# Three bfloat16 matmuls per token, of exact one-hots and split gates, in place of one float32 matmul

## The reference

```python
s1, i1 = lax.top_k(s[:, :, 0], PEER_TOPK)            # 16 best of 128 keys, first half
s2, i2 = lax.top_k(s[:, :, 1], PEER_TOPK)            # and second half
cand = (s1[..., :, None] + s2[..., None, :]).reshape(PEER_BLOCK, PEER_HEADS, PEER_TOPK * PEER_TOPK)
cidx = (i1[..., :, None] * PEER_NKEYS + i2[..., None, :]).reshape(PEER_BLOCK, PEER_HEADS, PEER_TOPK * PEER_TOPK)
top, pos = lax.top_k(cand, PEER_TOPK)
eidx = jnp.take_along_axis(cidx, pos, axis=-1)
gate = jax.nn.softmax(top, axis=-1)
a = jnp.einsum('thkd,td->thk', u_tab[eidx], xb).astype(jnp.float32)
act = (jax.nn.gelu(a) * gate).astype(xb.dtype)
return jnp.einsum('thk,thkd->td', act, v_tab[eidx])
```

## Time and profile before

| what | value |
|---|---|
| time, median of 3 runs | 1719.76 us (1716.88 to 1727.46) |
| profiled execution: span from the first to the last instruction | 1720.6 us |
| its mean granted TensorE clock | 0.990 of full speed |
| PE busy in it | 1674.9 us (97%) |
| DVE busy | 1178.9 us (69%) |
| POOL busy | 1124.5 us (65%) |

### The profile page before, as it was taken

The page is one execution under the profiler, slowest core; times in us unless marked ns, Lnnn a source line. Parts: engine busy times, 40 slices in busy tenths (PEclk is TensorE's granted clock), DMA queues, the critical chain, the costliest instruction groups (busy, mean ns, idle before and its releaser), DMA issues.

```text
span 1720.6 us, 27326 instructions
## 1 busy us (share of the span) xinstructions
PE 1674.9 (97%) x10559; PEld 1608.4 (93%) x10559; DVE 1178.9 (69%) x2324; ACT 665.7 (39%) x1059; POOL 1124.5 (65%) x677
## 2 busy tenths in 40 slices
PE   8999999899999999999999999999999999999996
PEld 3899878697999999999999999999999999999995
DVE  4340334645778799999787778446787887878755
ACT  2445222333334333334434433334444444444442
POOL 1677322132335888876766676778889799999952
PEclk9999999899999999999999999999999999999998
DMA  8544212034213999979999999979999999999951
GB/s 279 199 165 159 75 62 97 26 131 150 74 60 126 304 295 298 339 259 339 350 344 346 350 353 338 343 294 349 390 392 405 360 401 405 404 403 404 400 194 62
DMA packets 192705, 461.27 MB, mean 268 GB/s; under 512 B 21184, under 2 KB 99008, under 8 KB 192448
## 3 DMA queue, kind: packets, MB, share of 16 engines
q1 hardware_dynamic: 79872, 242.31, 39.4%
q0 software_dynamic: 46080, 167.79, 26.1%
q10 hardware_dynamic: 66624, 49.42, 8.7%
HBM read 407.64 MB, written 51.83 MB: 267 GB/s over the span
## 4 chain that ended last, share of the span: by engine, by line
PE 50%; DVE 4%; DMA 3%; POOL 1%; issue 1%; ACT 0%; DVEq 0%; SPq 0%; ACTq 0%
PE ps L922 44%; PE ps L933 5%; DMA tab<-in_tab 3%; POOL tLo L648 1%; DVE ug L1574 1%; POOL ug L658 0%; DVE ps L1584 0%; DVE yo L1820 0%; DVE eqb L1686 0%; DVE rs L1818 0%; DVE pick L1673 0%; DVE cand L1651 0%; DVE rs L1296 0%; DVE pos L1659 0%; PE ps L675 0%
## 5 line engine op out<-in xcount | busy, mean ns | idle before, releaser
L648 POOL TENSOR_TENSOR tLo<-tab,tHi 128x1024 fp32r<-128x1024 f32 x256 | 621.7, 2429 | 164.7 <-ACT tHi L1173 161.5
L1173 ACT CAST tHi<-tab 128x1024 fp32r<-128x1024 f32 x256 | 268.0, 1047 | 290.5 <-DMA tab<-in_tab 157.9
L922 PE MATMUL ps<-hHi,tLo 128*128 128x384 f32 x1024 | 352.0, 344 | 0.0
L922 PE MATMUL ps<-actHi,tLo 128*128 128x384 f32 x1024 | 342.7, 335 | 3.7 <-DVE actLo L1756 2.3
L922 PE MATMUL ps<-hHi,tHi 128*128 128x384 f32 x1024 | 345.7, 338 | 0.0
L922 PE MATMUL ps<-hLo,tHi 128*128 128x384 f32 x1024 | 344.8, 337 | 0.0
L922 PE MATMUL ps<-actLo,tHi 128*128 128x384 f32 x1024 | 342.1, 334 | 0.0
L922 PE MATMUL ps<-actHi,tHi 128*128 128x384 f32 x1024 | 342.1, 334 | 0.0
L636 POOL TENSOR_TENSOR wLo<-raw,wHi 128x1024 fp32r<-128x1024 f32 x53 | 128.2, 2418 | 292.1 <-ACT wHi L1004 292.1
L1574 DVE SCALAR_TENSOR_TENSOR ug<-ug,ps 128x1024 f32<-128x1024 f32 x160 | 191.0, 1218 | 48.3 <-DMA ug<-in_urows,eidx 47.1
L1584 DVE SCALAR_TENSOR_TENSOR ps<-ug,act_s,ps 128x1024 f32<-128x1024 f32 x158 | 202.5, 1282 | 5.0
(11 more groups left out here) (356 smaller groups left out, 2473.8 us busy)
## 6 DMA issues: line engine op xcount, KB each, us to landing
tab<-in_tab SPq DMA_DIRECT2D x256, 512.0 KB, 6.5
raw<-in_w SPq DMA_DIRECT2D x101, 512.0 KB, 3.7
gate_scratch<-stage ACTq DMA_DIRECT2D x48, 512.0 KB, 6.6
gt<-gate_scratch SPq DMA_DIRECT2D x32, 768.0 KB, 7.7
gelu_scratch<-ga ACTq DMA_DIRECT2D x112, 192.0 KB, 5.8
gin<-gelu_scratch SPq DMA_DIRECT2D x112, 192.0 KB, 11.0
ug<-in_urows,eidx POOLq DMA_INDIRECT x160, 6.7
ug<-in_vrows,eidx POOLq DMA_INDIRECT x160, 7.8
```

Source lines behind the costliest of these rows:

```text
L648: pool.tensor_tensor(tLo[:, n % SPL], tab[:, n % TABS], tHi[:, n % SPL].bitcast(F32), ALU.subtract).then_inc(s_tlo, 1)
L922: last = mm(ps[:, bank, 0:TD], w, x[:, k, 0:TD], start=first, stop=end)
L1173: nc.scalar.copy(tHi[:, n % SPL], tab[:, n % TABS]).then_inc(s_thi, 1)
```

## The change

The one-hots become bfloat16, in which 0, 1 and the key numbers are exact. Each gate is split into three bfloat16 pieces that add up to the float32 number (`gate3`; `gate_rest` holds what is left over). `w1` becomes `w3`, three products of `oh1` with a piece; PE adds the three matmuls of one token in PSUM. The layout of the one-hots turns from tokens x keys to keys x tokens, with the 8 tokens innermost, so that the operand that is repeated is repeated over the keys and its innermost run is 8 tokens. For PE the 128 columns of one token are therefore 8 elements (16 bytes) apart, in the weights and in the moving data; before they lay side by side. The key numbers (`key8`, repeated for 8 tokens), the chosen keys (`idx12`) and the gate pieces lie in SBUF now; nothing of the one-hots reads PSUM.

```diff
@@ gate_product (PE)
                     for t in range(4):
-                        last = mm(ps[:, GATE_BANKS[i % 3], t * P:(t + 1) * P], oh2[:, st % 2, 4 * part + t, :],
-                                  w1[:, st % 2, 4 * part + t, :], start=True, stop=True)
+                        for piece in range(3):
+                            last = mm(ps[:, GATE_BANKS[i % 3], t * P:(t + 1) * P], oh2[:, st % 2, :, 4 * part + t],
+                                      w3[:, st % 2, piece, :, 4 * part + t], start=(piece == 0), stop=(piece == 2))
                     last.then_inc(s_gmm, 1)
@@ preparation (DVE)
             for q in range(2):
                 nc.vector.tensor_copy(idx12[:, q], ps[:, 5 + q, 0:TD])
-            link(nc.vector.tensor_copy(oh1[:, 0:4, :], ps[:, 4, :].rearrange("p (t c) -> p t c", c=P)))
-            nc.vector.tensor_copy(iota_p, iota[:])
-            link(nc.vector.tensor_copy(g_cols[:], oh1[:, 0:3, :].rearrange("p t c -> p (t c)")))
+            nc.vector.tensor_copy(key8[:], over(iota[:], STEP_TOK))
+            link(nc.vector.tensor_copy(gate3[:, 0], ps[:, 4, 0:TD]))
+            link(tt(gate_rest[:], ps[:, 4, 0:TD], gate3[:, 0], ALU.subtract))
+            link(nc.vector.tensor_copy(gate3[:, 1], gate_rest[:]))
+            link(tt(gate_rest[:], gate_rest[:], gate3[:, 1], ALU.subtract))
+            link(nc.vector.tensor_copy(gate3[:, 2], gate_rest[:]))
@@ one_hots (DVE)
-                tt(oh2[:, st % 2], keys_, over(idx12[:, 1, at_], P), ALU.is_equal)
+                tt(oh2[:, st % 2], key8[:], along_keys(idx12[:, 1, at_]), ALU.is_equal)
                 if st:
                     v.wait_ge(s_oh, st)
-                link(tt(oh1[:], keys_, over(idx12[:, 0, at_], P), ALU.is_equal))
-                tt(w1[:, st % 2], oh1[:], over(g_cols[:, at_], P), ALU.mult).then_inc(s_oh, 1)
+                link(tt(oh1[:], key8[:], along_keys(idx12[:, 0, at_]), ALU.is_equal))
+                for piece in range(3):
+                    last = tt(w3[:, st % 2, piece], oh1[:], along_keys(gate3[:, piece, at_]), ALU.mult)
+                last.then_inc(s_oh, 1)
```

More of the change, by code:

```diff
@@ L280, in build @@
         ga = [at(f"ga{i}", [P, TD], (SPL_AT + 24576, SPL_AT + 24576 + 4 * TD, pos_sq + 6528)[i]) for i in range(3)]
-        idx12 = at("idx12", [P, 2, TD], SPL_AT + 27648)
+        gate3 = at("gate3", [P, 3, TD], SPL_AT + 27648, BF16)
         a_s = at("a_s", [P, NDOT], SPL_AT + 30720)
@@ L316, in build @@
         stage = peer("stage", [P, 2, NKEY, TB])
-        oh2 = peer("oh2", [P, 2, STEP_TOK, P])
-        w1 = peer("w1", [P, 2, STEP_TOK, P])
-        oh1 = at("oh1", [P, STEP_TOK, P], pos_sq + 1024)
+        gate_rest = at("gate_rest", [P, TD], zp[0])
+        oh2 = at("oh2", [P, 2, P, STEP_TOK], zp[0], BF16)
+        w3 = at("w3", [P, 2, 3, P, STEP_TOK], zp[0] + 4096, BF16)
+        oh1 = at("oh1", [P, P, STEP_TOK], pos_sq + 512, BF16)
+        key8 = at("key8", [P, P, STEP_TOK], pos_sq + 512 + 2048, BF16)
+        idx12 = at("idx12", [P, 2, TD], pos_sq + 512 + 4096, BF16)
+        assert 512 + 4096 + 4 * TD <= 3 * NST * PH * PK * 4
         zp[0] = Z_AT
@@ L350, in build @@
         h_rows = flat[:, 2 * 512:4 * 512]
-        g_cols = flat[:, 6 * 512:6 * 512 + TD]
-        iota_p = flat[:, 6 * 512 + TD:7 * 512]
         y_rows = h_rows
@@ L1720, in _, with along_keys @@
                 nc.vector.tensor_copy(idx12[:, q], ps[:, 5 + q, 0:TD])
-            link(nc.vector.tensor_copy(oh1[:, 0:4, :], ps[:, 4, :].rearrange("p (t c) -> p t c", c=P)))
-            nc.vector.tensor_copy(iota_p, iota[:])
-            link(nc.vector.tensor_copy(g_cols[:], oh1[:, 0:3, :].rearrange("p t c -> p (t c)")))
+            nc.vector.tensor_copy(key8[:], over(iota[:], STEP_TOK))
[4 more added lines that the diff above has]
+            link(nc.vector.tensor_copy(gate3[:, 2], gate_rest[:]))
             def one_hots(st):
                 at_ = slice(STEP_TOK * st, STEP_TOK * (st + 1))
-                keys_ = iota_p.unsqueeze(1).broadcast_to([P, STEP_TOK, P])
+                def along_keys(of_tokens):
+                    return of_tokens.unsqueeze(1).broadcast_to([P, P, STEP_TOK])
                 if st >= 2:
                     v.wait_ge(s_gmm, 2 * (st - 1))
-                tt(oh2[:, st % 2], keys_, over(idx12[:, 1, at_], P), ALU.is_equal)
+                tt(oh2[:, st % 2], key8[:], along_keys(idx12[:, 1, at_]), ALU.is_equal)
                 if st:
                     v.wait_ge(s_oh, st)
-                link(tt(oh1[:], keys_, over(idx12[:, 0, at_], P), ALU.is_equal))
-                tt(w1[:, st % 2], oh1[:], over(g_cols[:, at_], P), ALU.mult).then_inc(s_oh, 1)
+                link(tt(oh1[:], key8[:], along_keys(idx12[:, 0, at_]), ALU.is_equal))
+                for piece in range(3):
+                    last = tt(w3[:, st % 2, piece], oh1[:], along_keys(gate3[:, piece, at_]), ALU.mult)
+                last.then_inc(s_oh, 1)
             for st in range(NSTEP):
```

## The result

The changed kernel takes 1987.77 us (median of 6 runs, 1983.41 to 1996.11), the kernel before 1726.8 beside it: a ratio of 1.155, 95% interval 1.151 to 1.158. That is 188 us above the upper end of the range.

The account below looks back on a forecast made before the run. The prediction took PE's own work to bound the gate stage, its gate matmuls paced by weight loads. Profiled 1720.6 + 41.1 (gate matmuls) + 3.6 (start) = 1765.3 us, forecast 1765 us, range 1705 to 1800.

Parts of the forecast that it names:

- the price of a gate matmul: PE's gate steps: 24 bfloat16 matmuls at 0.107 us, 2.57 us in place of 1.71 a step, +41.1 us over 48.
- The gate matmuls are paced by their weight loads: PE's gate steps: loading 128 weight columns, not the columns that stream, sets the 0.107 us from one matmul to the next.
- rival A: PE's gate matmuls: bfloat16 weights load fast and 16-byte steps cost nothing; 0.060 us a matmul, 1711 us; chance 0.30.
- nearly half the rate: PE's 16-byte steps, priced from far-apart DVE output: half the rate for 128 columns taking 0.060 us is 0.12.
- Rival B: PE's gate matmuls: the layout slows the weight load itself to 0.214 us, +164 us, 1889 us; chance 0.12 (over 1800).
- 4.29 us a product: PE's product in a gate step: 4.29 us in the profile before, with no change to it in the sum.
- DVE's bfloat16 instructions: DVE's gate steps: five one-hot instructions at about 0.6 us, a step 5.4 us in place of 5.80, under PE's.
- D: DVE's one-hots miss the double rate as one operand is repeated: 8.1 us a step, 389 us; chance 0.12 with rival C.
- The preparation: DVE's work before the first gate step, with `key8` perhaps waiting for a POOL split: +3.6 us, once.
- PE didn't wait for DVE: Gate stage: PE waits for DVE's gate products at the first step, about 4 us, and hardly again.
- Rival C: Gate stage: POOL's splits hold up DVE's one-hots and make DVE the bound, +69 us, 1793 us; chance 0.12 with D.
- at least two hits per line: SBUF reads: full bandwidth wants two hits per 16-byte line; the new layout gives each column its own line; no price given.

Follow-up runs that it names:

- run 3: Changed kernel with only the weights read side by side, the moving data still 16 bytes apart (gates not the reference's): 1977.97 us.
- run 2: Changed kernel with only the moving data read side by side, the weights still 16 bytes apart (gates not the reference's): 1739.94 us.
- Run 1: Changed kernel with both weights and moving data read side by side (gates not the reference's): 1731.94 us, ratio 1.005 to the kernel before.
- 6: Changed kernel with the weights side by side and the moving columns 9 elements (18 bytes) apart in place of 8: 1982.32 us.
- 12: Changed kernel with every gate group cut in two, 12 matmuls behind the product and 12 in the middle of the next: 1976.66 us.
- 4: Changed kernel's computation with two tokens innermost, a token's columns 4 bytes apart in place of 16: 1737.09 us, ratio 1.0065 to the kernel before.
- 5: Changed kernel's computation with four tokens innermost, a token's columns 8 bytes apart in place of 16: 1774.53 us.
- run 7: Changed kernel's bfloat16 and three pieces with keys innermost: PE's columns side by side, DVE's repeated operand repeated in its innermost dimension: 1846.06 us.

## Why the prediction was wrong

**The step that failed is the price of a gate matmul**, "I take 0.107" with the upper end 0.214: it is 0.227, and 0.120 x 24 x 48 = 138 us of the error is that term. What the runs showed in its place: the moving data, read 16 bytes apart, set the pace (0.218 us with the weights side by side, run 3), and the weight load doesn't (0.063 with the weights alone apart, run 2). Both reasons behind it fell.

- "The gate matmuls are paced by their weight loads" fits the rows of the kernel before and was carried to bfloat16, where no row showed it. Run 1 has 24 loads at 0.055 us: bfloat16 loads of 128 columns hide under the streaming. That part of rival A was right. The Trainium skill ("TensorE: Matmul & The Clock Gate", Weight-path perf modes — Fast Weight Load (FWL) and DoubleRow) says that such loads go about twice as fast, and the 0.053 us that the prediction worked out from it as an estimate spoke against my 0.107. The trace of run 1, with a load and a matmul every 0.055 us, agrees.
- The layout was priced by a ratio. I read from the earlier trace rows that far-apart elements go at "nearly half the rate" and doubled the 0.060 us of a matmul. The same rows hold an absolute price, 1.8 ns an element; 128 of those are 0.23 us, and 1.77 ns a moving column was measured. That the two are one mechanism isn't shown, as the earlier trace rows are a DVE output with a step of 64 bytes and this is PE's input with 16; that the numbers come so near may be luck. But as an upper end it was the better choice, and the ratio had nothing to show that it carries over to PE.

Rival B had about the right number (0.214) for the wrong reason: it gave the slowness to the weight load. Run 3 leaves the weights side by side and stays at 0.218; run 2 leaves only them apart and is at 0.063.

**The term that was missing is the granted clock**: +80.7 us on products that the change doesn't touch, of which some 70 are matmuls at the low level. I took 4.29 us a product for fixed. Even rival B, with 0.227 for its 0.214, would have come to 1720.6 + 48 x (5.45 - 1.71) + 3.6 = 1904 us without this, 84 short. Runs 3, 6 and 12 show the low clock with the slow moving data, runs 1, 2, 4 and 5 a clock near 1.00 with the same number of matmuls; run 7 shows that waits of PE bring it down as well, but PE waits 3.7 us in the whole stage of the changed kernel. What in the slow matmuls brings the clock down isn't shown, only what PE did before it fell.

**The range** reached to 1800 and left rival B out with its 0.12; it should have reached B.

**What was right.** DVE's bfloat16 instructions take 0.68 us, and D didn't happen. (Its price was wrong all the same: run 7 makes it happen, and the stage takes 461 us and not 389, since DVE meets the splits on top.) The preparation cost 3.1 us (3.6 predicted), `key8` among it with 2.52 us beside a split, as worked out. PE didn't wait for DVE in the changed kernel (3.7 us, at the first step). Rival C was right as a mechanism: it is what happens as soon as the matmuls are repaired, and it eats the 16 us in runs 1 and 4. In the changed kernel it had no chance, as PE's stage left DVE 319 us to wait.

The Trainium skill ("SBUF — State Buffer", Door 1: The DMA port swizzle, its note on cachelines) says that one can stride for free as far as 16 bytes go, 8 bfloat16. The runs disagree for TensorE's moving data: 8 bytes cost double, 16 bytes four times, and only 4 are free. In the prediction I read "at least two hits per line" of the same page of the Trainium skill (Specifications (TRN2)) as the limit; with four tokens each 16 bytes hold two used columns, and it costs 0.114 us in place of 0.057.

## What to carry to other kernels

Before turning a layout for one engine's sake, bound the far-apart reads of the other one by the dearest price per element that a row shows, not by a ratio alone, and separately for each operand. Here an inner run of 2 bfloat16 kept VectorE's double rate and cost TensorE nothing, a run of 8 cost it four times. When one engine gets faster, look for what it had been hiding: shorter gate groups were worth nothing until VectorE, held by GpSimd's splits, had less to do. And slow matmuls can be paid twice, the second time by fast ones behind them, through the clock.

## What the runs showed of the hardware

- Moving data of bfloat16, 128 columns: 0.055 us side by side, 0.057 at 4 bytes from one to the next, 0.114 at 8, 0.227 at 16, 0.225 at 18. Weights at 16 bytes: 0.063 in place of 0.055.
- Gate matmuls with moving data 16 bytes apart come at the same distance at a granted clock of 1.00 and of 0.50 (0.235 us within a group); side by side they take 0.056 and 0.106. A PE that is busy without a gap, by the profile, still had its clock lowered, to a mean of 0.81 in the stage; the busy share of a row doesn't tell it.
- Splitting a GpSimd instruction of 2.4 us in four didn't reduce what VectorE loses to it (5.31 against 5.36 us a step).
